# Two weight-split and DMA placements at the start of a two-block layer kernel: tile 0 split before an eviction, identity loaded from the other queue

## The reference

```
x = x + 0.5 * swiglu(rms_norm(x, ffn1_norm), ffn1_w_gate_up, ffn1_w_down)

def rms_norm(x, g):
    xf = x.astype(jnp.float32)
    y = xf * lax.rsqrt(jnp.mean(xf * xf, axis=-1, keepdims=True) + EPS)
    return (y * g.astype(jnp.float32)).astype(x.dtype)

def swiglu(h, w_gate_up, w_down):
    a, b = jnp.split(h @ w_gate_up, 2, axis=-1)
    return (jax.nn.silu(a) * b) @ w_down
```

## Time and profile before

| what | value |
|---|---|
| median of 3 runs | 1463.88 us |
| profiled execution, its own time | 1463.48 us |
| span of its instructions | 1461.7 us |
| PE busy | 1451.7 us (99%) |
| PE weight loads busy | 1259.1 us (86%) |
| DVE busy | 983.4 us (67%) |
| ACT busy | 822.6 us (56%) |
| POOL busy | 152.1 us (10%) |
| HBM read | 265.36 MB |

### The profile page before, as it was taken

How to read it: one execution, slowest core, us unless ns; L and a number is a source line. 1 busy time by engine, 2 the same in 40 slices (tenths; PEclk the granted TensorE clock), 3 DMA queues, 4 the chain that set the end, 5 groups by cost and what they waited for, 6 DMA issues and landing times.

```text
span 1461.7 us, 20975 instructions
## 1 busy us (share of the span) xinstructions
PE 1451.7 (99%) x8088; PEld 1259.1 (86%) x8088; DVE 983.4 (67%) x1596; ACT 822.6 (56%) x1424; POOL 152.1 (10%) x219
## 2 busy tenths in 40 slices
PE   9999999999999999999999999999999999999999
PEld 7888888898888888888888988888887999888887
DVE  6666676676666666666776677666667756778775
ACT  6555556754555546555567646555467655466553
POOL 0200023000000001000050004000059100100000
PEclk9999999999999999999999999999999999999999
DMA  8765554454656546556564446655547334456551
GB/s 332 244 199 188 188 206 170 143 174 172 215 178 198 188 159 225 193 181 197 171 219 153 145 159 217 199 189 188 179 141 262 114 102 155 163 170 220 193 188 51
DMA packets 73683, 267.78 MB, mean 183 GB/s; under 512 B 8176, under 2 KB 8304, under 8 KB 73456
## 3 DMA queue, kind: packets, MB, share of 16 engines
q1 hardware_dynamic: 73296, 265.65, 54.4%
q10 hardware_dynamic: 288, 0.79, 0.1%
HBM read 265.36 MB, written 1.05 MB: 182 GB/s over the span
## 4 chain that ended last, share of the span: by engine, by line
PE 96%; DVE 1%; ACT 1%; issue 0%; DMA 0%; POOL 0%; DVEq 0%; POOLq 0%
PE bank L550 29%; PE bank L555 15%; PE bank L503 8%; PE bank L504 8%; PE bank L505 8%; PE bank L569 4%; PE bank L564 4%; PE bank L565 4%; PE bank L540 3%; PE bank L534 3%; PE bank L533 3%; PE bank L523 1%; PE bank L712 1%; PE bank L693 1%; PE bank L702 1%; DVE wlo L1562 1%
## 5 line engine op out<-in xcount | busy, mean ns | idle before, releaser
L1562 DVE TENSOR_TENSOR wlo<-raw,whi 128x1024 fp32r<-128x1024 f32 (+1 forms) x481 | 578.5, 1225 | 18.0 <-ACT whi L1031 18.0
L1031 ACT ACTIVATE whi<-raw 128x1024 fp32r<-128x1024 f32 (+1 forms) x481 | 497.6, 1050 | 5.2 <-PE bank L569 1.8
L550 PE MATMUL bank<-hx,whi 128*128 128x512 f32 x1856 | 470.4, 394 | 0.0
L550 PEld LDWEIGHTS bank<-hx,whi 128*128 128x128 f32 x1856 | 339.7, 188 | 64.4
L555 PEld LDWEIGHTS bank<-hx,wlo 128*128 128x128 f32 x1856 | 253.1, 190 | 18.4
L555 PE MATMUL bank<-hx,wlo 128*128 128x256 f32 x1856 | 258.7, 282 | 0.0
L503 PE MATMUL bank<-whi,hid 128*128 128x512 f32 x536 | 211.2, 394 | 0.2 <-issue 0.2
L504 PE MATMUL bank<-wlo,hid 128*128 128x512 f32 x536 | 209.9, 392 | 0.0
L505 PE MATMUL bank<-whi,hid 128*128 128x512 f32 x536 | 208.6, 389 | 0.0
L1060 ACT ACTIVATE hid<-prod 128x256 fp32r<-128x256 f32 x126 | 52.7, 418 | 169.1 <-DVE prod L1666 109.2
L505 PEld LDWEIGHTS bank<-whi,hid 128*128 128x128 f32 x536 | 100.7, 188 | 21.9
(11 more groups left out here) (259 smaller groups left out, 1601.2 us busy)
## 6 DMA issues: line engine op xcount, KB each, us to landing
raw<-w_dram SPq DMA_DIRECT2D x486, 512.0 KB, 4.1
gain<-g_dram SPq DMA_DIRECT2D x7, 512.0 KB, 3.6
arena<-c_dram SPq DMA_DIRECT2D x2, 768.0 KB, 6.7
cst<-c_dram SPq DMA_DIRECT2D x1, 1056.0 KB, 7.0
out_dram<-x SPq DMA_DIRECT2D x4, 256.0 KB, 2.0
par<-p_dram SPq DMA_DIRECT2D x1, 867.0 KB, 8.6
raw<-w_dram SPq DMA_DIRECT2D x2, 432.0 KB, 3.1
gain<-g_dram ACTq DMA_DIRECT2D x1, 512.0 KB, 4.8
```

What stands on the lines that cost most here:

```text
L550: e.matmul(b[:, :], hi_of(j)[:, k * P:k * P + P], hx[:, k * 2 * S:k * 2 * S + 2 * S], start=k == 0, stop=False, skip_group_check=True)
L1031: e.activation(hi_of(t), raw_of(t), ACT.Copy).then_inc(sem["w_hi"], 1)
L1562: e.tensor_tensor(lo_of(t), raw_of(t), hi_of(t).bitcast(F32), ALU.subtract).then_inc(sem["w_lo"], 1)
```

## The change

At the start of ACT's program the split of weight tile 0 is placed before both evictions of the turned input, which now follow each other. The load of the identity is taken out of SP's program and placed in ACT's, between the load of `xq(0, 1)` and the load of the gains. Lines behind the first place move up by one.

```diff
@@ sp_program
             e.dma_start(xq(0, 0), x_in[0:P, 0:512]).then_inc(sem["ld_x00"], 16)
-            e.dma_start(ident, const_in[:, 0:P]).then_inc(sem["ld_i"], 16)
             head = {STAGES[s]: T[f"{STAGES[s]}{HEADS.get(STAGES[s], 'p')}0"] for s in range(8)}
             for j in range(len(plan)):
                 load_tile(j)
@@ act_program
             e.dma_start(xq(0, 1), x_in[0:P, 512:1024]).then_inc(sem["ld_x01"], 16)
+            e.dma_start(ident, const_in[:, 0:P]).then_inc(sem["ld_i"], 16)
             e.dma_start(gain[:, :], gains[0]).then_inc(sem["ld_gain"], 16)
             E.wait_ge("mh", 1)
             e.activation(small[:, 12:13], mhalf[:, 0:1], ACT.Square)
             squares(0, 0, 0)
-            norm_hi(0, 0, (0,))
             hi_upto(0)
-            norm_hi(0, 0, (1,))
+            norm_hi(0, 0)
             hi_upto(1)
             squares(0, 1, 0)
             squares(0, 1, 1)
```

## The result

The changed kernel takes 1466.91 us (median of 14 runs, 1465.92 to 1467.69) against 1463.34 us before (14 runs): the ratio is 1.0023, 95% interval 1.0015 to 1.0030. It is slower by 3.6 us. The profiled execution took 1466.46 us with a span of 1464.7. It lies 0.45 us under its median, and the profiled one of before 0.14 over its own, so the profiles show 3.0 of the 3.6 us.

A forecast was written before the change was run, and what follows sets the result against it. TensorE holds 96% of the chain of waits, so only its start was taken to matter. 0 for the split plus 0.9 for the gains took 1463.48 to 1464.4, as a median 1464.8 us, range 1463.1 to 1465.9.

The forecast's parts named there:

- What bounds the kernel: Chain of waits: TensorE holds 96%, so only the moment from which it runs without a pause can move the time.
- the mark: TensorE's first product on tile 3, at 16.45 us before; shifts there were taken over to the end one for one.
- The split worth 0: ScalarE's split of tile 0, moved into idle time, gains 0 since tile 1 lands at 10.18; ends 0 and -0.84.
- The direction and the cause: Start of the kernel: the gains land later and release VectorE's norm; +0.2 to +1.6 us, +0.9 taken, chance 0.60.
- same: Whole kernel's time: an effect under 0.2%, 2.9 us, that can't be told from none; chance 0.95.
- The gains' landing: Gains' DMA on ScalarE's queue: landing moves from 5.96 to between 7.6 and 8.9 us, 8.3 taken.
- Landings follow the bytes ahead of them: DMAs at the start: one stream, a landing set by KB issued up to it, 1600 KB at about 7.6 us.
- s: Start of VectorE's norm, 6.55 before; the mark comes at s + 9.06, unmoved while s is under 7.39; 8.35 taken.
- The even sharing of the queues: Rival at the DMA queues: gains move beside tile 0, both end at 7.6 or before; about +0.1 us, chance 0.20.
- The clock: Rival: TensorE's clock falls in the gap before the transposes; 3.2 us counted, 1468.0 with the gains, chance 0.05.
- a sign of being wrong: TensorE's products of 128 x 512 following each other at 0.43 us, among the observations that would refute the prediction.
- The 9.06 us from norm to mark: Sum of intervals in the earlier trace, from the norm's start over evictions and splits to TensorE's first product on tile 3.

The follow-up runs named there:

- the tiny load: Kernel before with one more DMA, 16 partitions of 64 B, on ScalarE's queue ahead of the gains: 1467.62 us against 1463.38, ratio 1.0031.
- the longer warm-ups: Changed kernel with 27 products of zeros at the start instead of 15: 1466.04 us; also with the second half's squares ahead of the evictions: 1465.63 us.
- the fillers: Changed kernel with two DMAs of 16 partitions of 32 B on SyncE's queue between the first input and tile 0: 1466.51 us, ratio 1.0023.
- the three parts: Changed kernel with the identity loaded in 128-partition pieces, two on SyncE's queue ahead of tile 0, one on ScalarE's ahead of the gains: 1466.67 us, ratio 1.0023.

## Why the prediction was wrong, step by step

- **What bounds the kernel: right.** Both edits act on the stretch up to the mark; after it nothing is won or lost (mark +2.85, span +3.0).
- **The split worth 0: right**, with the reason given: with it alone ScalarE waits for tile 1, and the time is 0.9999 of before.
- **The direction and the cause: right.** The gains come late, the norm is released by their DMA, and the identity's line carries all of the loss. But I gave 0.95 to "same", within 0.2% and not to be told from none. The interval is only 0.08% to either side, and the loss is clear of none. The forecast also stood on a median of three executions, 1463.88; fourteen give 1463.34, so the effect was missed by more than the times alone say (+3.6 us measured, +0.9 forecast).
- **The gains' landing: the step that failed.** "Landings follow the bytes ahead of them" gave 7.6 to 8.9 and I took 8.3; they land at 9.35. With 9.35 in the place of 8.3 the sum is s = 9.46 and 18.52 at the mark, +2.1 instead of +0.9. The rule holds for SyncE's stream (the input's second half at 8.7, tile 1 at 10.0) and, with SyncE's later loads held back, for the gains too (7.47, where I had 7.6 for it). My upper bound was the landing of the input's second half, for which I had no reason but that the two are issued together. In the trace it lands first and the gains 0.7 us behind it, since SyncE's queue gets 222 packets to the gains' 128 and goes on to tile 1 while they wait.
- **The even sharing of the queues: partly right.** I gave 0.20 to it and priced it at +0.1. The packets do take turns after the change, 74 against 73 and then 52 against 46, as the Trainium skill says (DMA: Bandwidth & Descriptors, Queues, rings and completion order). But turns by packet are not turns by byte, so in this trace the small identity lasted as long as the whole of tile 0, with the gains behind it; that it is not needed for the loss, the version with the tiny load shows. The stretch of the earlier trace rows still isn't explained by it: there tile 0 was issued at 1.63 and had its first packet at 4.88.
- **The clock: wrong in chance, and in price.** I gave it 0.05 and 3.2 us. It fell, once TensorE's idle time grew from 0.8 to 3.5 us, a gap I had put at 2.6, and the products of 128 x 512 follow each other at 0.43 us (13.65, 14.08), which I had named as a sign of being wrong. (The warm-up's pace I had misread: 7 and 11 count the products that touch the stretch, of which 5 and 8 start in it. They start 0.21 and 0.11 us apart, so what I took from it stands.) The low clock costs 0.3 to 0.9 us, since the slow products lie mostly under ScalarE's and VectorE's work: the transposes delay the second eviction by 0.7, and 0.6 of it reaches the split of tile 1.
- **The 9.06 us from norm to mark: too short.** In the changed kernel it is 9.84 (19.30 - 9.46): the low clock moves the split of tile 1 by 0.6, and TensorE, still behind with its products, reaches the mark 2.08 behind the norm of the second half (17.22) instead of 1.88. With the clock held it is 9.47: I had added it up from a trace in which GpSimd's root lay in a gap of VectorE, and there the root takes the place of the clock.

The account of the 2.85 us at the mark: 18.52 - 16.45 = 2.07 from the gains by the old chain, and 19.30 - 18.52 = 0.78, which I read as the clock's. GpSimd has no part in it: its root ends at 16.50, and the norm of the second half starts at 17.22 behind VectorE's own work. GpSimd comes in once the clock is held, so taking the low clock away gives back 0.3 at the mark and not 0.78.

**Left open:** why the gains are late when they are third on ScalarE's queue. In seven versions with the gains third and SyncE going on, they landed at 8.8 to 9.7: 9.35 in the change, 9.2 with the identity alone, 9.4 and 9.5 with the longer warm-ups, 9.7 behind the tiny load, 8.8 with the fillers and 9.4 with the three parts. Second, they landed at 6.0, or at 7.6 beside tile 0; third with SyncE's later loads held back, at 7.47. The place and the time of issue are not separated: in every version with the gains third they were also issued at 1.64 instead of 1.17, and the run that was to issue them late in second place issued them at 1.22. That the place is the cause is not shown. Three of these runs show the 16 DMA engines together well under 400 GB/s while several issued DMAs are waiting, so bytes and turns alone don't explain it. How the work of a DMA reaches the engines was not measured.

## What to carry to other kernels

At the start of a program count for each queue which DMA is first, second and third, and look at what a small load would be put ahead of: it can cost more than its bytes, here 3.35 us at the gains' landing for 64 KB. In this kernel the gains were in time only where they were second on their queue and issued before tile 0. Before closing a gap of one engine, look at who works in it.

## What the runs showed of the hardware that I had not expected

- Two DMAs on two queues took turns by packets, not by bytes: 128 packets of 512 B lasted as long as 128 of 4 KB (landings at 6.33 and 6.15). The turns were not always even: 222 packets of 4 KB went on SyncE's queue while the gains' 128 of the same size went on ScalarE's.
- The gains, third on ScalarE's queue, were late in each version in which SyncE went on issuing, whether 1, 16 or 64 KB stood directly before them. With three small DMAs early the 16 engines carried 147 to 184 GB/s from 4 to 5 us instead of 404, and some engines finished a DMA over 3 us behind others (5.3 to 8.8 us with the fillers).
- GpSimd's operations on 128 x 1 values take 0.30 and 0.56 us alone and 0.85 to 1.01 and 1.44 to 1.60 (four versions) beside VectorE's subtraction of two operands in SBUF. The Trainium skill (SBUF — State Buffer, Who interferes with whom) names the port pair that the two engines share as the one place of contention; these rows agree.
- TensorE's granted clock fell to 0.50 in an idle time of 3.5 us that followed 5.8 us of products, and in another version at 10.13, near the end of the transposes that followed an idle time of 1.9 us. In the changed kernel it was back 5.5 us after the transposes began.
